# A hybrid encoder trunk on one core: two first weight chunks streamed in quarters side by side, and the last rows' scaling shared out over three engines

## The reference

```python
p = x @ attn_w_in[j]                      # XQ, QK and V columns
recalled = _memory_attention(p[..., 3 * MIX_W:], mem, mem_w_kv[layer])
y = jnp.concatenate([mixed, recalled], axis=-1) @ w_o[layer]
x = _layer_norm(ALPHA * x + y, ln_gain[layer, 0], ln_bias[layer, 0])
f = _conv_ffn(x, ffn_w_up[layer], ffn_conv[layer], ffn_w_down[layer])
x = _layer_norm(ALPHA * x + f, ln_gain[layer, 1], ln_bias[layer, 1])
# _layer_norm: (x - mean) * rsqrt(var + eps) * gain + bias
```

## Time and profile before

| | us |
|---|---|
| median of 3 runs (lowest, highest) | 1250.84 (1249.69, 1251.08) |
| the profiled execution's own time | 1250.47 |
| its span in the trace | 1248.7 |
| TensorE busy | 1235.7 (99% of the span) |
| VectorE busy | 1024.2 (82%) |
| ScalarE busy | 729.7 (58%) |
| GpSimd busy | 20.0 (2%) |

### The profile page before, as it was taken

One profiled execution on the slowest core, in us unless ns is written; L12 is line 12 of the kernel. 1 busy time (PEld: TensorE's weight loads), 2 busy tenths in 40 slices (PEclk: granted clock), 3 DMA queues, 4 the chain that ended last, 5 costly groups with the idle time before them and its releaser, 6 DMA issues.

```text
span 1248.7 us, 19664 instructions
## 1 busy us (share of the span) xinstructions
PE 1235.7 (99%) x7368; PEld 1082.9 (87%) x7368; DVE 1024.2 (82%) x1597; ACT 729.7 (58%) x1188; POOL 20.0 (2%) x29
## 2 busy tenths in 40 slices
PE   8999999999999999999999999999999999999997
PEld 6888888888999998888889888888888888888886
DVE  6776888888879888988888878988888776988887
ACT  6665755555776546655554545655554774755552
POOL 0000000000000000000000000000000000000000
PEclk9999999999999999999999999999999999999999
DMA  9744575556454345666555665665555533666651
GB/s 337 236 146 135 183 245 187 190 186 191 154 185 133 121 137 168 224 197 200 188 187 169 221 204 168 221 202 189 192 189 172 188 119 118 204 218 202 193 193 54
DMA packets 64106, 229.27 MB, mean 184 GB/s; under 512 B 7526, under 2 KB 9190, under 8 KB 62860
## 3 DMA queue, kind: packets, MB, share of 16 engines
q1 hardware_dynamic: 64012, 228.02, 55.6%
HBM read 226.93 MB, written 1.06 MB: 183 GB/s over the span
## 4 chain that ended last, share of the span: by engine, by line
PE 95%; DMA 2%; DVE 1%; ACT 1%; SPq 0%; issue 0%; DVEq 0%
PE pair L753 28%; PE acc L853 21%; PE pair L756 14%; PE pair L791 4%; PE pair L792 4%; PE pair L793 4%; PE acc L753 2%; PE acc L834 2%; PE acc L832 2%; PE acc L833 2%; PE pair L1012 2%; DMA raw<-in_stream 1%; PE pair L816 1%; PE pair L820 1%; PE pair L818 1%; PE acc L756 1%
## 5 line engine op out<-in xcount | busy, mean ns | idle before, releaser
L1266 DVE TENSOR_TENSOR w_lo<-raw,w_hi 128x1024 fp32r<-128x1024 f32 x402 | 485.3, 1222 | 108.7 <-ACT w_hi L1030 107.2
L1030 ACT ACTIVATE w_hi<-raw 128x1024 fp32r<-128x1024 f32 x402 | 422.7, 1058 | 216.5 <-PE pair L756 69.8
L753 PE MATMUL pair<-xT,w_hi 128*128 128x512 f32 x1520 | 478.3, 396 | 1.5 <-ACT bias_rows L1193 1.5
L756 PEld LDWEIGHTS pair<-xT,w_lo 128*128 128x128 f32 x1520 | 285.8, 188 | 66.8
L756 PE MATMUL pair<-xT,w_lo 128*128 128x256 f32 x1520 | 298.9, 278 | 0.0
L753 PEld LDWEIGHTS pair<-xT,w_hi 128*128 128x128 f32 x1520 | 233.9, 189 | 4.9 <-issue 2.0
L1077 ACT ACTIVATE hid<-pair 128x512 f32<-128x512 f32 x88 | 52.5, 596 | 125.0 <-PE pair L756 125.0
L791 PE MATMUL pair<-xT,w_hi 128*128 128x256 f32 x344 | 100.3, 292 | 0.0
L1307 DVE TENSOR_TENSOR hid<-pair,hid 128x512 f32<-128x512 f32 x88 | 60.7, 690 | 47.3 <-ACT hid L1077 47.2
L792 PE MATMUL pair<-xT,w_hi 128*128 128x256 f32 x344 | 97.4, 283 | 0.0
L793 PE MATMUL pair<-xT,w_lo 128*128 128x256 f32 x344 | 97.3, 283 | 0.0
(11 more groups left out here) (221 smaller groups left out, 1661.1 us busy)
## 6 DMA issues: line engine op xcount, KB each, us to landing
raw<-in_stream SPq DMA_DIRECT2D x402, 512.0 KB, 4.6
gains<-in_ln SPq DMA_DIRECT2D x8, 1024.0 KB, 8.3
bias<-bias_scratch SPq DMA_DIRECT2D x2, 1152.0 KB, 8.6
x_tok<-in_x_t SPq DMA_DIRECT2D x4, 256.0 KB, 5.2
raw<-in_stream SPq DMA_DIRECT2D x4, 256.0 KB, 5.4
y_tok<-in_mem_t SPq DMA_DIRECT2D x1, 1024.0 KB, 10.2
x_tok<-in_x SPq DMA_DIRECT2D x1, 1024.0 KB, 6.7
out<-x_tok SPq DMA_DIRECT2D x4, 256.0 KB, 2.0
```

What stands on the lines that cost most here:

```text
L753: pe.matmul(bank, w_hi[:, slot, kk * P:(kk + 1) * P], xT[:, kk].rearrange("p a s -> p (a s)"), start=(kk == 0), stop=(kk == KT - 1), skip_ ...
L756: last = pe.matmul(bank[:, 0:SEQ], w_lo[:, slot, kk * P:(kk + 1) * P], xT[:, kk, 0, :], start=False, stop=(kk == KT - 1), skip_group_check ...
L1030: nc.scalar.activation(w_hi[:, u % SPLIT, :], raw[:, u % RAW, :], ACT.Copy).then_inc(hi_ready, 1)
L1266: v.tensor_tensor(w_lo[:, u % SPLIT, :], raw[:, u % RAW, :], w_hi[:, u % SPLIT, :].bitcast(F32), ALU.subtract).then_inc(lo_ready, 1)
```

## The change

Chunks 0 and 1 (XQ and QK0) are streamed together: each quarter of the input is followed by a quarter of chunk 0 and one of chunk 1, 12 transfers of 256 KB in all, instead of 8 of them and units 2 and 3. The layout of the stream's first two chunks follows suit. TensorE does the quarters of both chunks in turn. One more idle product of 256 columns is added before them. `bias_rows` moves ahead of chunk 1's last quarter, the cuts of the memory move ahead of unit 8, and `xexp` 1 moves ahead of unit 14. In the last norm, tile 1: VectorE does `centre` for both halves and `scale` for half 1; ScalarE multiplies half 0 by 1/sqrt(var), and GpSimd adds the bias to it; SyncE sends half 1 before half 0.

```diff
@@ make_schedule
     for q in range(4):
-        items.extend([("cut", "x", q), ("begin", q)])
-    for u in range(2, AHEAD):
-        split_units(u)
+        items.extend([("cut", "x", q), ("begin", q, 0), ("begin", q, 1)])
...
         if layer == 0:
             split_units(1 + AHEAD)
+            items.append(("bias_rows",))
...
-                at[0], at[2] = [("bias_rows",)], [("cut", "mem", q) for q in range(4)]
-                at[5] = [("prepare",)]
+                at[1], at[5] = [("cut", "mem", q) for q in range(4)], [("prepare",)]
+                at[8].remove(it("xexp", 1))
+                at[7].append(it("xexp", 1))
@@ sync
                 sp.dma_start(x_tok[:, q // 2, at], xT_dram[:, q // 2, at]).then_inc(xT_landed[q], 16)
-                sp.dma_start(raw[:, q // 2, at], stream[0, :, q * 512:(q + 1) * 512]).then_inc(
-                    raw_landed[q // 2] if q % 2 else first_landed[q // 2], 16)
-            for u in range(2, RAW):
-                if u == RAW - 1:
-                    for dst, src in small[:2]:
-                        sp.dma_start(dst[:], src).then_inc(table_landed, 16)
+                for u in (q // 2 * 2, q // 2 * 2 + 1):
+                    sp.dma_start(raw[:, u, at], stream[u // 2, :, u % 2 * UNIT + at.start:u % 2 * UNIT + at.stop]).then_inc(
+                        raw_landed[u] if q % 2 else first_landed[u], 16)
+            for dst, src in small[:2]:
+                sp.dma_start(dst[:], src).then_inc(table_landed, 16)
+            for u in range(4, RAW):
                 load_unit(u)
...
-            for t in range(TT):
-                for h in range(2):
+            for t, h in ((0, 0), (0, 1), (1, 1), (1, 0)):
                     at = slice(h * 512, (h + 1) * 512)
-                    sp.wait_ge(x_ready, x_count(2 * DEPTH - 1, t, h))
+                    if (t, h) == (1, 0):
+                        sp.wait_ge(last_added, 1)
+                    else:
+                        sp.wait_ge(x_ready, x_count(2 * DEPTH - 1, t, 0 if t else h))
@@ tensor
+                elif c < 2:
+                    for q, b in {(0, 0): [(0, 0), (0, 1), (1, 0), (1, 1)], (0, 1): [(2, 0), (2, 1), (3, 0)], (1, 0): [(3, 1)],
+                                 (1, 1): [(3, 1)]}[c, i]:
+                        for w, a in {(1, 0): HI, (1, 1): LO}.get((c, i), HI + LO):
+                            last = first_products(q, b, w, a)
...
             idle_work(WARM_UP)
+            pe.matmul(ACC[0][:, 0:SEQ], zeros[:, 0:P], zeros[:, 0:SEQ], start=True, stop=True)
@@ scalar
+                elif name == "norm" and item[1:] == (2 * DEPTH - 1, 1):
+                    act.wait_ge(centred, 1)
+                    act.wait_ge(rstd_ready, TT * 2 * DEPTH)
+                    nc.scalar.activation(y_tok[:, 1, 0:512], y_tok[:, 1, 0:512], ACT.Copy, scale=rstd[:, 1:2]).then_inc(last_scaled, 1)
@@ vector, norm
+                    if (m, t) == (2 * DEPTH - 1, 1):
+                        v.scalar_tensor_tensor(y_tok[:, t, 0:512], ACC[2 * t][:], mean_var[:, t, 0:1], gains[:, 0, 0:512],
+                                               ALU.subtract, ALU.mult).then_inc(centred, 1)
+                        centre(1)
+                        dve.wait_ge(rstd_ready, TT * m + t + 1)
+                        scale(1)
+                        continue
@@ gpsimd
+                if name == "norm" and item[1:] == (2 * DEPTH - 1, 1):
+                    pool.wait_ge(last_scaled, 1)
+                    nc.gpsimd.tensor_tensor(x_tok[:, 1, 0:512], y_tok[:, 1, 0:512], gains[:, 1, 0:512], ALU.add).then_inc(last_added, 1)
```

More of the change, by code:

```diff
@@ L472, in trunk_kernel @@
         xT_landed = [sem(f"xT_landed{q}") for q in range(4)]
-        first_landed = [sem("first_landed0"), sem("first_landed2")]
+        first_landed = [sem(f"first_landed{u}") for u in range(4)]
         cut_hi, cut_lo = [{"x": sem(f"x_{name}"), "mem": sem(f"mem_{name}")} for name in ("hi", "lo")]
@@ L500, in trunk_kernel @@
         dve_step, pool_step = sem("dve_step"), sem("pool_step")
+        centred, last_scaled, last_added = sem("centred"), sem("last_scaled"), sem("last_added")
         scratch = nc.dram_tensor("bias_scratch", [HEADS, 512], F32, kind="Internal").ap()
@@ L679, in logits_banks, with first_products @@
                 return ACC[2 * (n % 2)], ACC[2 * (n % 2) + 1]
+            HI, LO = [(w_hi, xT_hi), (w_hi, xT_lo)], [(w_lo, xT_hi)]
+            def first_products(q, b, w, a):
+                slot, n = 2 * (q // 2) + b, 2 * (q // 2) + b + 1
+                if w is w_lo:
+                    pe.wait_ge(*(lo_ready, n) if q % 2 else (first_lo, n))
+                else:
+                    pe.wait_ge(*(hi_ready, n) if q % 2 else (first_hi, n))
+                    pe.wait_ge((cut_hi if a is xT_hi else cut_lo)["x"], q + 1)
+                for k in (2 * q, 2 * q + 1):
+                    for j in range(2):
+                        at = (k % 4 * 2 + j) * P
+                        last = pe.matmul(PROJ[b][:, j * SEQ:(j + 1) * SEQ], w[:, slot, at:at + P], a[:, k, :],
+                                         start=(w is w_hi and a is xT_hi and k + j == 0),
+                                         stop=(w is w_lo and k == KT - 1), skip_group_check=True)
+                return last
             def half(c, i, pos, begun=False):
@@ L686, in half @@
                 held = form == "O" and index[0] == chunks_of_sum - 2
-                if (c, i) == (1, 0):
-                    pe.wait_ge(hi_ready, 3)
-                elif c:
+                if c > 1:
                     pe.wait_ge(lo_ready, 2 * c + (2 if final or c in early else i + 1))
@@ L1147, in _ @@
                 elif name == "begin":
-                    u, h = item[1] // 2, item[1] % 2
+                    u, h = item[1] // 2 * 2 + item[2], item[1] % 2
                     at = slice(h * 512, h * 512 + 512)
@@ L1604, in _ @@
                 name = item[0]
-                if name == "stats":
+                if name == "norm" and item[1:] == (2 * DEPTH - 1, 1):
+                    pool.wait_ge(last_scaled, 1)
+                    nc.gpsimd.tensor_tensor(x_tok[:, 1, 0:512], y_tok[:, 1, 0:512], gains[:, 1, 0:512], ALU.add).then_inc(last_added, 1)
+                elif name == "stats":
                     m, t = item[1], item[2]
@@ L1647, in stream_layout @@
         cols = {"QK": (P * index, MIX + P * index), "CG": (MIX + P * index, 2 * MIX + P * index)}.get(role)
-        if c == 0:
-            stream[c] = w[:, col:col + 256].reshape(KT, P, 256).transpose(1, 0, 2).reshape(P, 2 * UNIT)
+        if c < 2:
+            for i, first in enumerate(cols or (col, col + P)):
+                block = w[:, first:first + P].reshape(2, KT // 2, P, P).transpose(2, 0, 1, 3)
+                for h in range(2):
+                    stream[h].reshape(P, 2, KT // 2, 2, P)[:, c, :, i] = block[:, h]
             continue
```

## The result

The changed kernel took 1254.48 us (median of 15 runs, lowest 1253.45) against 1250.84 for the kernel before (15 runs): a ratio of 1.0030, 95% interval 1.0023 to 1.0037. That is 3.6 us slower, where 1.5 was forecast and 1253.4 was the upper end of the range. The experiments ran on three chips, where the kernel before took 1250.5 (runs 1 to 4), 1250.68 (5 to 8) and 1250.76 (9 to 12); the changed kernel was timed again on the first of them alone, 1254.5.

What follows compares the result with a forecast made beforehand. TensorE, 99% busy, was taken as the bound, so its shift after the start-up waits plus the tail decides: +1.2 and +0.3 make 1.5 us, 1252.3 us against the median, range 1249.8 to 1253.4.

Steps and rivals of the forecast that it cites:

- The start: Up to KM: QK1 starts at 18.8 us, KM at 27.7 instead of 29.17; 1.45 us gained if only this counted.
- The swap: `xexp` 1 ahead of unit 14: 0.95 us won at the second `log`, but `xpv` 0 later; +1.2 us.
- TensorE's wait of some 2 us: Sign at `xprobT`, near 59.3 us, before `xpv` 0: TensorE waits some 2 us there and nowhere later.
- The tail: Last norm, tile 1: VectorE's `scale` 1 and GpSimd's add exclude each other, so the split costs +0.3 us.
- The second gate: VectorE at `prepare` until `lam_w`, the last table, lands: left at 38.87 us, bounds 0.3 earlier and 2.1 later.
- the 39.9: Sign at `masks`, expected at 38.9 us: the prediction is wrong if it comes before 37.7 or after 39.9.
- rival 2: Slower by over 0.2%: unit 13 asked for late, transfer engines run dry, `lam_w` 1.4 us late; 1253.7 us; chance 0.08.

Runs made afterwards that it cites:

- run 4: The kernel before with only the swap: `xexp` 1 moved ahead of unit 14; 1251.83 us, ratio 1.0012.
- run 6: The changed kernel with the four cuts of the memory back behind unit 8; 1252.66 us, ratio 1.0018.
- run 7: The changed kernel without the swap, with the old tail, and `prepare` moved behind the second half of QK3; 1248.35 us, ratio 0.9984.
- run 9: The changed kernel with the last two small tables issued ahead of unit 13 instead of behind units 13 and 14; 1248.88 us, ratio 0.9984.
- run 1: The changed kernel once more, no edit; 1254.5 us, ratio 1.0030.
- run 12: The kernel of run 7 with the cuts of the memory back behind unit 8; 1251.43 us, ratio 1.0005.
- run 2: The changed kernel without the swap, `xexp` 1 behind unit 14 again; 1255.4 us, ratio 1.0037.
- run 11: The changed kernel with GpSimd's add also waiting for VectorE's last `scale`; 1254.36 us, ratio 1.0028.
- run 3: The changed kernel with the last norm and the order of output transfers of the kernel before; 1253.38 us, ratio 1.0025.

## Why the prediction was wrong, step by step

**The start held in the main.** QK1 was put at 18.8 and KM at 27.7 behind some 3 us of waiting; they came at 19.38 and 27.27, behind 2.2. KM is 1.90 us earlier, beyond the 1.2 to 1.6 that were allowed; the two misses, 0.6 later and 0.4 earlier, had no effect, since the gate came after them.

**The swap held.** +1.2 was forecast, 1.23 is measured in both settings, and `exp` 0 and `xpv` 0 are late by just the forecast amounts once the gate's shift is taken off: 1.53 and 1.23. The match of `exp` 0 to 1.51 is closer than its sum: 1.78 less 0.19 is 1.59. TensorE's wait of some 2 us came in two parts, 0.63 us at L937, the transposes of `xturn` 0, and 1.28 at L957: 1.9 in all, in the changed kernel as in run 4. The prediction had it all at L957.

**The tail held.** +0.3, with the add ending 1.13 us after `scale` 1 (forecast 1.07) and 1.26 long alone (forecast 1.23).

**The second gate failed.** "The bytes ahead of `lam_w` are the same, so I leave 38.87 where it is; its bounds are 0.3 us earlier [...] and 2.1 later": that term was +2.2, just past its upper bound, and `masks` at 41.09 is past the 39.9 that the prediction had named as a sign of being wrong. Its own bounds gave 1.2 + 2.1 + 0.3 = 3.6 us, 1254.4; the range stopped at a table 1.1 us late. The bytes are the same, but unit 13's were asked for late, and the engines were not full meanwhile (run 6). `lam_w` was issued 0.5 us later than before (31.12 against 30.61, where 0.3 sooner was forecast) and took longer to land, as the row of its transfer says (KB, us from issue to landing), where before it was 8.2:

```profile
lam_w<-in_lam SPq DMA_DIRECT2D x1, 256.0 KB, 9.9
```

The traces with either start and the tables in their old place show that it is no scatter: `masks` at 38.87, 39.70, 38.40 and 38.64 with the old start, 41.09, 41.76, 41.66 and 40.61 with the new one and early cuts. In run 7, where `prepare` no longer waits, `lam_w` landed at 39.6 (30.88 + 8.7) with unit 13 asked for at 27.98, so the size of the delay is not fixed. This was rival 2, with the place (unit 13 asked for late) and the mechanism (engines no longer full) right, and its price of 1.4 and its chance of 0.08 too low. The argument against it was that 28.8 plus the shortest landing of 3.6 is early enough. That asks when unit 13 lands; what counted is whether the engines stay full until it is asked for. Run 6 shows it: unit 13 on time, 1.8 us back. Run 9 shows what the gate as a whole is worth: `lam_w` ahead of unit 13, 5.6 back. Of the 2.2, 0.4 remain in run 6, which is within the scatter of the gate; whether the slower first transfers have a part in them stays open.

**What was also missed.** The lead of 1.9 us at KM was not there to be lost at the gate alone. From KM to `xlog` are 8.80 us before (29.17 to 37.97), 8.79 in run 7 and 10.28 in the changed kernel (27.27 to 37.55): after the wait of 2.2 us the granted clock was 0.50 from 29 to 31 us. It cost 1.5 us that the gate hid, in full, in the changed kernel. In run 9's profiled execution (1250.19 us, where the median is 1248.88), which has the same 10.28, nothing hid it. The executions of run 7 fall into two groups that differ by about as much: seven at 1247.3 to 1248.4 us with a mean granted clock of 0.998 to 1.000, four at 1249.5 to 1250.3 with 0.997.

## What to carry to other kernels

When an edit moves work ahead of the release of a buffer, follow that release to the transfer that it allows, and ask whether the transfer engines still have enough to do until the late issue; that the sum of bytes is the same says nothing. A small table that gates a whole engine belongs ahead of the bulk transfers, or its consumer belongs later: the first edit won 5.6 us from the changed kernel, the second 1.3 from the kernel before, where the whole new start brought 1.0 more (the medians do not tell 1.3 from 1.0). And gains in front of a gate are worth nothing until it is moved: the early cuts cost 1.8 us with the gate in place (run 1 against 6) and won 3.1 without it (run 7 against 12, part of it by the clock). The best versions are run 7, 1248.35 us, and run 9, 1248.88; the two edits together were not tried.

## What the hardware showed that was not expected

After waits of 2.0 to 2.3 us before KM the granted clock fell to its lower level for some 3 us in the changed kernel and in runs 2, 9 and 11 (10.27 to 10.28 us from KM to `xlog`), and stayed at 1.00 in runs 3 and 7 (8.79) after a wait just as long. The stretch 29 to 31 us of the changed kernel, then of run 7 (the granted clock is the third number from the end):

```profile
29.00:31.00 2.00, 2.00 (x11) 2.00 (x11) 1.94 (x4) 1.06 (x1) 0.00 (x0) 0.50 1.01 350
```
```profile
29.00:31.00 2.00, 2.00 (x19) 2.00 (x18) 1.89 (x4) 1.35 (x2) 0.00 (x0) 1.00 1.01 365
```

Eleven products against nineteen in the same 2 us. After 3.9 us (run 6) and 5.3 us (run 12) the clock fell as well: 10.28 and 10.93 us. The wait of 1.04 us before had no such effect. So in this kernel a wait of about 2 us is a lottery that costs 0 or 1.5 us; what decides it no run here shows. The Trainium skill, "TensorE: Matmul & The Clock Gate", section "Part 1: The HAM clock gate (the "warmup" mystery)", gives the two levels as 1.2 and 2.4 GHz, and the trace agrees: 0.50 is half of the full clock.

SyncE's issues do not all take the same time. In the changed kernel the tenth took 1.84 us, where the first took 0.39. Nine had been issued by then; that the number on their way is the reason is likely, but was not tested:

```profile
0.74 0.39 SPq L606 DMA_DIRECT2D x_tok<-in_x_t  x1
...
4.97 1.84 SPq L606 DMA_DIRECT2D x_tok<-in_x_t  x1
6.85 1.41 SPq L608 DMA_DIRECT2D raw<-in_stream  x2
8.30 0.55 SPq L611 DMA_DIRECT2D onehot<-in_onehot_c  x1
```

The small tables behind them went out at 8.30 instead of 6.05. `bias_rows`, which needs them, still ran at 16.89 us on TensorE (16.71 before), so it cost nothing here.
